# Two transformer blocks in split float32 on one core: tiles begin at multiples of 1024 bytes, and the opening's modulation runs on four column groups

## What is computed

```
sh1, sc1, gt1, sh2, sc2, gt2 = split(silu(c) @ w_ada + b_ada, 6)         # w_ada is 1024 x 6144
csh1, csc1, ... = split(silu(c_ctx) @ w_ada + b_ada, 6)
hc = rmsnorm(ctx, g_pre_mix) * (1 + csc1) + csh1                         # 256 tokens
hx = rmsnorm(x, g_pre_mix) * (1 + sc1) + sh1                             # 512 tokens
yx = token_mixers(hx @ w_in, ...)        # gated linear attention in two directions, and a short convolution
x  = x + gt1 * rmsnorm(yx @ w_out, g_post_mix)
x  = x + gt2 * rmsnorm((silu(conv(h @ w_u)) * (h @ w_g)) @ w_down, g_post_ffn)
```

## Time and profile before

| | |
|---|---|
| median of 3 runs | 1497.46 us (1496.51 to 1503.56) |
| profiled execution | 1501.94 us |
| its span, first to last instruction | 1500.2 us |
| granted TensorE clock, mean | 0.966 of 2.4 GHz |
| busy: TensorE, its weight loads, DVE, ACT, GpSimd | 94%, 75%, 60%, 27%, 56% |
| DMA | 142.05 MB, mean 95 GB/s |

### The profile page before, as it was taken

How to read it: one execution, slowest core, us unless ns; L and a number is a source line. 1 busy time by engine, 2 the same in 40 slices (tenths; PEclk the granted TensorE clock), 3 DMA queues, 4 the chain that set the end, 5 groups by cost and what they waited for, 6 DMA issues and landing times.

```text
span 1500.2 us, 19664 instructions
## 1 busy us (share of the span) xinstructions
PE 1415.0 (94%) x6922; PEld 1130.2 (75%) x6922; DVE 897.7 (60%) x1268; ACT 399.0 (27%) x751; POOL 834.9 (56%) x651
## 2 busy tenths in 40 slices
PE   6899888999879999999998999999799999999998
PEld 4467666877748888888887888776488888888887
DVE  4459868775466666662007589744664888887000
ACT  2342222332242222221002312255522333332000
POOL 0224333442647666667775577533166777777765
PEclk9889899998989999999999999999899999999999
DMA  9437721211212333333332233211122333333332
GB/s 313 135 93 252 210 54 43 57 57 43 85 28 88 96 97 98 98 94 88 104 93 75 79 98 89 81 57 43 29 83 86 98 98 91 96 93 91 102 91 81
DMA packets 224315, 142.05 MB, mean 95 GB/s; under 512 B 5595, under 2 KB 210944, under 8 KB 224256
## 3 DMA queue, kind: packets, MB, share of 16 engines
q1 hardware_dynamic: 222389, 140.11, 31.5%
q10 hardware_dynamic: 1867, 1.12, 0.3%
HBM read 139.12 MB, written 2.10 MB: 94 GB/s over the span
## 4 chain that ended last, share of the span: by engine, by line
PE 80%; DVE 12%; issue 2%; ACT 2%; DMA 1%; POOL 1%; SPq 0%; ACTq 0%; DVEq 0%; POOLq 0%
PE ps L518 24%; PE ps L520 23%; PE ps L519 23%; DVE ada_acc L1646 2%; PE ps L558 2%; DVE g_z L1747 1%; DVE norm_acc L1578 1%; PE ps L771 1%; PE ps L1012 1%; PE ps L1028 1%; PE ps L1041 1%; PE ps L599 1%; DMA par_rows<-in_conv_w 1%; DVE xT L1997 1%; DVE SS L1829 1%
## 5 line engine op out<-in xcount | busy, mean ns | idle before, releaser
L481 POOL TENSOR_TENSOR w_lo<-raw,w_hi 128x1024 fp32r<-128x1024 f32 x213 | 535.3, 2513 | 17.8
L518 PE MATMUL ps<-h_hi,w_hi 128*128 128x512 f32 x1064 | 428.0, 402 | 16.4 <-DVE h_lo L1600 10.1
L519 PE MATMUL ps<-h_lo,w_hi 128*128 128x512 f32 x1064 | 419.7, 394 | 0.0
L520 PE MATMUL ps<-h_hi,w_lo 128*128 128x512 f32 x1064 | 419.3, 394 | 0.0
L477 POOL TENSOR_TENSOR w_hi<-raw,cst 128x16 fp32r<-128x16 f32 x213 | 63.4, 298 | 618.2 <-PE ps L520 552.3
L518 PEld LDWEIGHTS ps<-h_hi,w_hi 128*128 128x128 f32 x1064 | 202.9, 191 | 70.7 <-issue 21.2
L520 PEld LDWEIGHTS ps<-h_hi,w_lo 128*128 128x128 f32 x1064 | 202.7, 191 | 43.9
L519 PEld LDWEIGHTS ps<-h_lo,w_hi 128*128 128x128 f32 x1064 | 203.2, 191 | 39.9
L478 POOL TENSOR_SCALAR w_hi<-raw 128x1008 fp32r<-128x1008 f32 x213 | 230.2, 1081 | 0.0
L1918 DVE SCALAR_TENSOR_TENSOR f_acc<-ps,par,f_acc 128x441 f32<-128x441 f32 (+2 forms) x176 | 122.3, 695 | 48.9 <-ACT f_acc L1115 25.1
L518 PE MATMUL ps<-f_hi,w_hi 128*128 128x512 f32 x352 | 138.3, 393 | 0.2 <-POOL w_lo L481 0.2
(11 more groups left out here) (284 smaller groups left out, 1983.0 us busy)
## 6 DMA issues: line engine op xcount, KB each, us to landing
raw<-in_w_up SPq DMA_DIRECT2D x88, 512.0 KB, 3.9
raw<-in_w_in SPq DMA_DIRECT2D x59, 512.0 KB, 4.0
raw<-in_w_down SPq DMA_DIRECT2D x32, 512.0 KB, 3.8
v_tok<-in_w_ada SPq DMA_DIRECT2D x18, 512.0 KB, 6.3
ada_first<-in_w_ada SPq DMA_DIRECT2D x8, 1024.0 KB, 11.7
raw<-in_w_out SPq DMA_DIRECT2D x16, 512.0 KB, 3.7
ada<-in_w_ada SPq DMA_DIRECT2D x14, 512.0 KB, 5.5
raw<-in_w_down SPq DMA_DIRECT2D x16, 384.0 KB, 3.5
```

Source lines behind the costliest of these rows:

```text
L481: pool.tensor_tensor(w_lo[:, slot % 2, :], raw[:, slot, :], w_hi[:, slot % 2, :].bitcast(F32), ALU.subtract).then_inc(S("lo_split"), 1)
L518: nc.tensor.matmul(dst, lhs_hi, rhs_hi, start=first, stop=False)
L519: nc.tensor.matmul(dst, lhs_hi, rhs_lo, start=False, stop=False)
L520: return nc.tensor.matmul(dst, lhs_lo, rhs_hi, start=False, stop=last)
```

## The change

Five things are changed; the products themselves and everything from the third unit on are the same instructions.

1. **Addresses.** `cst` moves behind `w_lo`, `small` in its place; `token_root` and `token_rinv` become one tile; `cst` grows by two columns. By the declared sizes `raw` begins at 39,936, `w_hi` at 56,320, `w_lo` at 64,512, `h_hi` at 78,848, `norm_sq` at 111,616, `f_hi` at 125,952: all multiples of 1024.
2. **Modulation on four column groups.** The conditions are kept in `cond_wide`, 32 columns per tile of channels with 30 of them zero. The eight matmuls of a pair go to four groups of 32 PSUM partitions in turn; the four partial sums are added when the row is turned, by a matmul with the new constant `pick`.
3. **Order of the opening.** The conditions have a small load of their own and are turned first. The four pairs of the scale come first, then those of the shift; each pair of the shift is turned as soon as it is there, in rows of 256, and `h_hi`, `h_lo` of two tiles can then be made. Pairs seven and eight, their rows and the context's sum stand between the products of unit 0 (`between_products`).
4. **The context** is loaded behind six pairs, copied out of PSUM by ACT, and its squares have buffers of their own (`squares_of`).
5. **Queues.** ACT's loads of masks, head norms, sinks and positions go to SP, behind unit 4; parameter rows on ACT come after the conditions; the constants are loaded in two parts.

```diff
@@ tiles
     xT = sb("xT", [P, KT, T])
-    cst = sb("cst", [P, CONST_COLS])
+    small = sb("small", [P, 96])
     masks = sb("masks", [P, len(LEVELS), P], I32)
...
     w_lo = sb("w_lo", [P, 2, 1024], F32R)
+    cst = sb("cst", [P, CONST_COLS])
...
-    small = sb("small", [P, 96])
...
-    token_root, token_rinv = sb("token_root", [P, 7, 4]), sb("token_rinv", [P, 7, 4])
+    token_stat = sb("token_stat", [P, 2, 7, 4])
+    token_root, token_rinv = token_stat[:, 0], token_stat[:, 1]
...
+    TURN_BANKS = [0, 1, 6, 7, 0, 1, 6, 7, 0, 1, 6, 1, 6, 1]
+    PAIR_ORDER = [4, 5, 6, 7, 0, 1, 2, 3]
+    PAIR_BANKS = {4: 2, 5: 2, 6: 4, 7: 4, 0: 5, 1: 2, 2: 4, 3: 1}
@@ sync
+        for i, n in enumerate(PAIR_ORDER):
+            if i >= FIRST_SLOTS:
+                sp.wait_ge(S("ada_first_used"), i - FIRST_SLOTS + 1)
...
+            if i == 3:
+                load_unit(0, 0, columns(w_in, COL_AF)(0))
+            elif i == 5:
+                sp.dma_start(x_tok[:, CHUNKS:, :], a["ctx"].rearrange("(t p) d -> p t d", p=P)).then_inc(S("ctx_loaded"), 16)
+            elif i == 6:
+                load_unit(1, 1, columns(w_in, COL_K)(0))
...
                     if u0 + i == 3:
-                        sp.wait_ge(S("ada_turned"), 1)
+                        sp.wait_ge(S("ada_turned"), 5)
...
+                    if u0 + i == 4:
+                        sp.dma_start(masks[:, :, :], a["masks"]).then_inc(S("masks_loaded"), 16)
...
@@ tensor
+        def ada_pair(i):
+
+            n = PAIR_ORDER[i]
+            pe.wait_ge(ada_first_loaded[i % FIRST_SLOTS], 16 * (i // FIRST_SLOTS + 1))
             for t in range(KT):
-                mm = nc.tensor.matmul(ps[0:2, 2 + n // 2, (n % 2) * 256:(n % 2) * 256 + 256], cond[:, t, :],
-                                      ada_first[:, n % FIRST_SLOTS, t, :], start=(t == 0), stop=(t == KT - 1))
+                j = t % 4
+                mm = nc.tensor.matmul(ps[32 * j:32 * j + 32, PAIR_BANKS[n], (n % 2) * 256:(n % 2) * 256 + 256], cond_wide[:, t, :],
+                                      ada_first[:, i % FIRST_SLOTS, t, :], start=(t < 4), stop=(t >= 4), skip_group_check=True)
...
+        def between_products(at):
+
+            if at == 2:
+                ada_pair(6)
+            elif at == 3:
+                turn_row(4)
+            elif at == 4:
+                pe.wait_ge(S("ctx_turned"), 4)
+                ada_pair(7)
                 sum_squares(1, TC)
+            elif at == 5:
+                turn_row(5)
+            elif at == 8:
                 spread(1, TC, "rinv_ready")
...
+        for _ in two_units(0, 0, (0, 2), between_products):
             pass
@@ scalar
+        for m in range(4):
+            x_shifted(m)
+        for i in range(4):
+            act.wait_ge(S("turned"), 11 + i)
+            activate(ctxT[:, 2 * i:2 * i + 2, :].rearrange("p k t -> p (k t)"), ps[:, TURN_BANKS[10 + i], :], ACT.Copy).then_inc(S("ctx_turned"), 1)
+        for m in range(KT):
+            square(1, m, lambda m: ctxT[:, m, :], lambda m: act.wait_ge(S("ctx_turned"), m // 2 + 1), TC)
+        copy_row(4)
+        x_shifted(4)
+        x_shifted(5)
+        root(1, TC)
+        copy_row(5)
+        x_shifted(6)
+        x_shifted(7)
```

More of the change, by code:

```diff
@@ new lines, in turn_row @@
+        def turn_row(i):
+            pe.wait_ge(S("ada_rows"), i + 1)
+            if i == 3:
+                pe.wait_ge(S("mod_ready"), 1)
+            tiles = range(8 + 4 * i, 12 + 4 * i) if i < 2 else range(2 * (i - 2), 2 * (i - 2) + 2)
+            for r, m in enumerate(tiles):
+                mm = nc.tensor.matmul(ps[:, ROW_BANKS[i], 2 * m:2 * m + 2], v_tok[:, i, r * P:(r + 1) * P], const("pick", 2), start=True, stop=True)
+            if i >= 1:
+                mm.then_inc(S("ada_turned"), 1)
@@ L636, in _ @@
                 spread(1, TC, "rinv_ready")
-        for m in range(16):
-            if m % 4 == 0:
-                pe.wait_ge(S("ada_rows"), m // 4 + 1)
-            mm = nc.tensor.matmul(ps[:, 2, 2 * m:2 * m + 2], v_tok[0:2, m // 4, (m % 4) * P:(m % 4 + 1) * P],
-                                  cst[0:2, CONST["ident"]:CONST["ident"] + 2], start=True, stop=True)
-        mm.then_inc(S("ada_turned"), 1)
         def gates(c):
@@ new lines, in _, with copy_row, x_shifted @@
+        load_par_rows(act, 0)
+        def copy_row(i):
+            act.wait_ge(S("ada_first_used"), 2 * i + 2 if i < 2 else i + 3)
+            bank, first, end = ROW_PARTS[i]
+            activate(v_tok[:, i, 0:end - first], ps[:, bank, first:end], ACT.Copy).then_inc(S("ada_rows"), 1)
+        for m in range(KT):
+            square(0, m, lambda m: xT[:, m, :], lambda m: act.wait_ge(S("turned_out"), m + 1))
+        root(0)
+        for i in range(4):
+            copy_row(i)
+        def x_shifted(m):
+            act.wait_ge(S("shift_ready"), m // 2 + 1)
+            shifted(0, m, h_hi, lambda m: mod[:, m, 0:1])
@@ L1612, in _, with add_bias @@
         add_squares(0)
+        for n in range(8, 10):
+            turned_out(n)
+        vec.memset(gw[:, :], 0.0).then_inc(S("gw_cleared"), 1)
+        vec.memset(al[32:33, :], 1.0).then_inc(S("gw_cleared"), 1)
         invert(0)
-        add_squares(1, TC)
-        invert(1, TC)
+        def add_bias(tiles, bank):
+            return vec.tensor_tensor(mod[:, tiles, :], ps[:, bank, 2 * tiles.start:2 * tiles.stop].rearrange("p (m i) -> p m i", i=2),
+                                     column("b_ada", tiles.start, tiles.stop - tiles.start).unsqueeze(2)
+                                     .broadcast_to([P, tiles.stop - tiles.start, 2]), ALU.add)
         dve.wait_ge(S("ada_turned"), 1)
-        order.done(vec.tensor_tensor(mod[:, 0:16, :], ps[:, 2, 0:32].rearrange("p (m i) -> p m i", i=2),
-                                     column("b_ada", 0, 16).unsqueeze(2).broadcast_to([P, 16, 2]), ALU.add))
+        order.done(add_bias(slice(8, 16), ROW_BANKS[0]))
         order.wait()
```

197 lines of the change are left out of this document (107 added, 90 removed).

## The result

| | before | after |
|---|---|---|
| median, 4 runs each | 1496.99 us (1495.65 to 1503.56) | 1477.71 us (1475.81 to 1479.79) |
| profiled execution | 1501.94 us | 1479.79 us |
| its span | 1500.2 us | 1478.0 us |

The ratio is 0.9863, 95% interval 0.983 to 0.9896: 19 us or 1.4% faster. The forecast was 1432 us, 65 us faster, with a range of 1420 to 1482. The time lies inside the range, but it is rival B's (1476), not the forecast's: the opening gave what it was to give, the addresses nothing.

The account below looks back on a forecast made before the run. TensorE, busy 94% of the span, was taken as the bound, the triple product holding 70% of the chain. From 1501.9 profiled, -21 (opening) and -45 (addresses) gave 1436; the median 4.5 lower, 1432 us, range 1420 to 1482.

Parts of the forecast that it names:

- rival B: Tile addresses do nothing, the 32 cycles lie between one stream and the next; opening gain alone, 1476 us; chance 0.33.
- The addresses: -45 us: Triple products on the chain: tiles at multiples of 1024 save 11.0 ns on each of 4250, 45 us in all.
- A: The forecast itself: both the opening and the addresses gain, 1420 to 1448 us; chance 0.50.
- Rival D: Opening fails: groups do not overlap or row 4 waits longer, and addresses do nothing; about 1492 to 1500 us; chance 0.05.
- Rival E: Slower: stationary and moving operands begin alike in a block, two readers meet, 13.3 ns more per product; 1533 us; chance 0.05.
- Opening: -21 us: Start of the kernel up to the gates: new order and column groups gain 21 us, ends -27 and -14.
- (2): Opening, scale half: its last pair lands near 23 us; turning its rows fits in the waits for the next pairs.
- (3): Opening, modulation pairs on four column groups: 1.5 us each with the clock low, against 3.6 now.
- (4): Opening, after pair six: two rows and four ctx turns, the last two waiting for ACT; first product at 39, not 68.85.
- (5): Opening, unit 0: TensorE waits after four steps for row 4, behind DVE's adds of 8 us; goes on at 47 or 48.
- (6): Opening, remaining 36 products, pairs 7 and 8 and sums until 60; two context units 5.8 us; gates at 66, not 88.19.
- (7): Behind the opening: w_ada pieces issued near 50, not 65.57; five small loads on SP's queue cost 1 us.

Follow-up runs that it names:

- pace_read: Changed kernel with feed-forward operands replaced: one column streamed 0.216 us apart, dense bf16 stream 0.216, one column as all stationary near 0.229, one column both sides 0.216.
- pace_place: Changed kernel, feed-forward products cut: stream from 4 bytes on 233.3 ns apart, from 16 bytes 226.9; 126 stationary columns from 4 bytes 232.7; 64 stationary columns 230.0.
- pace_start: Changed kernel, feed-forward streams starting later, all ending at the tile's end: from 16 bytes 226.7 ns apart, 32 bytes 226.8, 8 bytes 230.1, 64 bytes 226.7.
- one_group: Changed kernel with all eight matmuls of a pair sent to the same 32 partitions, new order kept: 1493.76 us, ratio 0.9975 to the kernel before.
- addr_only: Kernel before with only the new order of tiles (and two more columns in cst): 1497.06 us against 1498.2, ratio 0.9999.
- pace_kind: Changed kernel, other operands in the feed-forward products: 64 rows 226.7 ns apart, 384 columns 173.4, high halves as bf16 two elements apart 224.8, 32 stationary columns 231.6.
- pace_columns: Changed kernel, feed-forward widths from the tile's start: 480 columns 216.7 ns apart, 496 columns 223.4, 500 columns 225.3; 124 stationary columns from 16 bytes on 226.7.
- low_bf16: Changed kernel with low parts of the activations stored as dense bf16, only their product changed: 1500.32 us against 1500.33 for the kernel before, ratio 1.001.

## Why the prediction was right in one part and wrong in the other

**"The addresses: -45 us" is the step that failed**: it measured 0 (2.5 us at most either way). The observation under it was right: 13.3 ns in both 512 and 256 columns, none at half clock (426.6 ns for 512 columns at 0.50), little in two-pass products (2.3 to 2.7 ns), weight loads innocent (191 and 189 ns). Even the place was right, the reading of the stream: 10.7 ns (`pace_read`), against the 11.0 of the term. What failed is the sentence "A stream that begins inside a block touches one block more": a whole stream of 4-byte elements has the same 13.3 ns whether it begins 32 bytes past a multiple of 1024 or on one. All tiles of before lay 32 past a multiple of 128, so no row could tell the two apart, and I gave A 0.50 where the rows stood evenly for A and B. The runs show a smaller grain: in `pace_place` and `pace_start` starts 4 and 8 bytes past cost 6 to 7 and 3.4 ns and a start 16 past does not, and by the declared sizes the operands of all these products begin at multiples of 16, before and after. The 3.3 ns of the 496 columns from 64 bytes on such a grain does not explain.

**Rival B** got its time right (1476 against 1477.71, and 1480.38 for the opening alone) with only half of its reason: the 32 cycles (13.3 ns at 2.4 a nanosecond) do belong to this kind of product, but not "between one stream and the next"; that part is 2.7 ns. **Rival D** had the groups fail and the time at 1492 to 1500; `one_group`, where they are left out, gives 1493.76. **Rival E**, two readers that meet at equal starts, did not happen: the products of `addr_only` are 0.227 us apart.

**"Opening: -21 us"** was right: 21.2 at the gates and 22.0 at the end by these two traces (20.3 and 16.3 against the trace of `addr_only`), 19 by the medians. Its steps one by one:

- (1) Landing of the sixth pair, forecast 31.4: the two pairs done at 30.35 + 1.93 = 32.3. Right. DMA moved 339 GB/s.
- (2) The rows of the scale are turned at 21.34 and 29.37, between pairs, as forecast; the fourth pair was through at 28.6, not near 23. DVE waited 8.5 us for its row, but its four scaled tiles were done at 33.7, as the shift's first row came, so the first product lost nothing by it.
- (3) A pair 1.5 us: 1.07 at full clock, 1.5 to 1.93 where the clock was low (0.68 from 44.4 to 45.8 us, 0.50 from 23 to 25). Right, and `one_group` shows that this term holds 13 of the 21 us at the gates; the prediction's end for groups that do not overlap, -14 in place of -21, was too mild (8 earlier at the gates, 4 at the end).
- (4) First product 39: 41.53. I counted four turns of ctx that wait for four `h_hi` in a row. In fact ACT's third `h_hi` waited another 2.93 us for DVE's second bias, which stands behind two `h_lo` and two scaled tiles. A wait of one engine for another that in turn serves a list was missed.
- (5) "I price them at 8 us: TensorE goes on at 47 or 48": the seven adds took 3.61 us, from 43.15. GpSimd had split unit 1 by 39.4, before them, and did nothing beside them; beside those of the earlier trace rows it was busy for 7.46 of the 8.96 us. No wait of 4 us was left: pair 7 filled the time, and row 4 was turned at 46.61. The late first product and the short adds offset one another: that the gates came out within 1 us of the forecast is in part luck.
- (6) Products of the unit until 60: 58.94. The context 5.8 us: 7.6, as its products wait for `hc_lo` 0.2 us at a time. Gates 66: 67.01.
- (7) Pieces near 50: 51.34. Whether SP's small loads cost the one us can't be told: the lead grew from 21.2 to 22.0 against one trace of the old opening and fell from 20.3 to 16.3 against the other.

The timeline after, of ACT (the wait for the second bias), DVE (the adds) and SP's queue:

```profile
38.04 1.33 ACT L1177 ACTIVATE h_hi<-norm_sq,mod 128x512 fp32r<-128x512 f32 x2 [2.93 <-DVE mod L1698]
...
43.15 3.61 DVE L1656 TENSOR_TENSOR norm_root<-norm_root,norm_rinv 128x256 f32<-128x256 f32 x7 [1.01 <-ACT norm_rinv L1177]
...
51.34 0.88 SPq L427 DMA_DIRECT2D ada<-in_w_ada  x2
```

## What to carry to other kernels

A constant in the trace that fits a hypothesis is evidence for it only if some row has the other value of what the hypothesis turns on; where all tiles begin at the same offset, one product with a shifted operand is cheaper than a term of 45 us in a sum. Follow one instruction through both traces: it says where a lead arises and where it is kept. But do it with two traces of the old kernel, for here two traces of the old opening parted by 4 us in a stage behind it. And small matmuls with few stationary columns are worth spreading over column groups where they stand in a chain (13 us at the gates here), while mending a single wait in a list that three engines serve may only uncover the next.

## What the runs showed of the hardware that I had not expected

- The distance of one-pass products with 512 columns at full clock depends on what the stream is made of: 226.7 ns with different 4-byte elements, 224.8 with bf16 two elements apart, 216 with dense bf16 or one element repeated (`pace_kind`, `pace_read`).
- Fewer stationary columns are not faster but slower: 226.7 with 128 or 124 (`pace_columns`), 230.0 with 64 (`pace_place`), 231.6 with 32 (`pace_kind`), though the weight loads shrink from 188 to 134 and 109 ns.
- A step float32r, bf16, float32r takes 0.700 us, 31 ns more than its three products take in stages of their own kind (`low_bf16`).
- Eight float32 matmuls of 256 columns on four groups of 32 columns take 1.07 us (`after`, 13.19 us) instead of 3.6, less than a third. The earlier trace rows had shown plain float32 on two groups.
